# A hybrid encoder layer on one core: the first token tile of the row projection multiplies by the high parts of the weights first and by the low parts behind, with the second tile's first group between

## What is computed

```
h = rms_norm(x, g_pre_mix)
proj = h @ w_in.astype(x.dtype)
qa, ka, va, za, aa, ba, qb, kb, vb = jnp.split(proj, _split_points(IN_SPLITS), axis=-1)
...
mix = jnp.concatenate([o_a, o_b], axis=-1) @ w_out.astype(x.dtype)
x = x + rms_norm(mix, g_post_mix)
h = rms_norm(x, g_pre_ffn)
u = causal_depthwise_conv(h @ w_up.astype(x.dtype), ffn_conv_w) + ffn_conv_b.astype(x.dtype)
gate, val = jnp.split(u, 2, axis=-1)
y = (jax.nn.gelu(gate, approximate=True) * val) @ w_down.astype(x.dtype)
return x + rms_norm(y, g_post_ffn)
```

## Time and profile before

| | us |
|---|---|
| median of 3 runs | 1221.24 |
| lowest and highest | 1220.97, 1221.99 |
| the profiled execution's own time | 1222.27 |
| its span in the trace | 1220.2 |
| PE busy | 1168.4 (96%) |
| DVE busy | 803.5 (66%) |
| ACT busy | 540.3 (44%) |
| POOL busy | 395.1 (32%) |
| mean granted TensorE clock, share of full speed | 0.99 |

### The profile page before, as it was taken

One profiled execution on the slowest core, in us unless ns is written; L12 is line 12 of the kernel. 1 busy time (PEld: TensorE's weight loads), 2 busy tenths in 40 slices (PEclk: granted clock), 3 DMA queues, 4 the chain that ended last, 5 costly groups with the idle time before them and its releaser, 6 DMA issues.

```text
span 1220.2 us, 16966 instructions
## 1 busy us (share of the span) xinstructions
PE 1168.4 (96%) x5964; PEld 987.4 (81%) x5964; DVE 803.5 (66%) x1135; ACT 540.3 (44%) x973; POOL 395.1 (32%) x353
## 2 busy tenths in 40 slices
PE   6999999998899999988699999999999999999997
PEld 5888888887888888876488888888888878888886
DVE  6333345467866677758678787787877867664457
ACT  5221143556355444435455444444444434653451
POOL 1222000211133332223346765557655561000001
PEclk9999999999999999999799999999999999999999
DMA  7322224446232223231144535445355557997613
GB/s 267 127 78 86 68 86 121 143 140 227 82 115 88 92 71 116 64 104 55 69 138 138 188 131 199 168 143 191 130 196 172 173 179 254 363 374 235 191 60 138
DMA packets 118292, 181.85 MB, mean 149 GB/s; under 512 B 20527, under 2 KB 78671, under 8 KB 113999
## 3 DMA queue, kind: packets, MB, share of 16 engines
q1 hardware_dynamic: 118223, 180.94, 44.1%
HBM read 123.21 MB, written 57.70 MB: 148 GB/s over the span
## 4 chain that ended last, share of the span: by engine, by line
PE 48%; DVE 3%; issue 1%; ACT 1%; POOL 0%; DVEq 0%; POOLq 0%; ACTq 0%
PE sums L2912 6%; PE sums L2913 6%; PE sums L2914 6%; PE f_ps_up L2912 6%; PE f_ps_up L2913 5%; PE f_ps_up L2914 5%; PE f_ps_up L2985 3%; PE f_ps_up L2986 3%; PE f_ps_up L2984 3%; PE sums L2986 2%; PE sums L2985 2%; PE sums L2984 2%; DVE h_t L2798 0%; ACT stage L2606 0%; DVE f_rest_raw L2695 0%
## 5 line engine op out<-in xcount | busy, mean ns | idle before, releaser
L2866 POOL TENSOR_TENSOR f_w_raw<-stage 128x512 f32<-128x512 f32 x44 | 69.4, 1578 | 136.5 <-PE f_ps_up L2914 132.8
L2620 DVE TENSOR_TENSOR f_w<-f_w_raw,f_w 128x512 fp32r<-128x512 f32 (+1 forms) x55 | 71.0, 1310 | 23.6 <-POOL f_w_raw L2866 23.5
L2870 POOL TENSOR_TENSOR conv<-conv 128x512 f32<-128x512 f32 x44 | 73.0, 1658 | 16.9 <-DMA conv<-in_w_down 14.3
L222 PE MATMUL sums<-split,slab_w 128*128 128x512 f32 x192 | 75.9, 395 | 0.5 <-PEq L273 0.5
L2870 POOL TENSOR_TENSOR f_conv<-f_conv 128x512 f32<-128x512 f32 x44 | 65.4, 1486 | 32.0 <-DMA y_blocks<-f_conv 28.6
L224 PE MATMUL sums<-split,slab_w 128*128 128x512 f32 x192 | 74.9, 390 | 0.0
L223 PE MATMUL sums<-split,slab_w 128*128 128x512 f32 x192 | 74.7, 389 | 0.0
L2912 PE MATMUL f_ps_up<-split,f_w 128*128 128x512 f32 x176 | 69.5, 395 | 4.4 <-DVEq L2616 3.7
L243 DVE SCALAR_TENSOR_TENSOR conv<-sums,conv_taps,conv 128x1023 f32<-128x1023 f32 (+6 forms) x39 | 46.8, 1199 | 37.3 <-ACT conv L234 36.4
L2913 PE MATMUL f_ps_up<-split,f_w 128*128 128x512 f32 x176 | 69.2, 393 | 0.0
L2914 PE MATMUL f_ps_up<-split,f_w 128*128 128x512 f32 x176 | 69.1, 393 | 0.0
(11 more groups left out here) (410 smaller groups left out, 3462.9 us busy)
## 6 DMA issues: line engine op xcount, KB each, us to landing
stage<-in_w_up SPq DMA_DIRECT2D x22, 1024.0 KB, 6.0
y_blocks<-f_conv SPq DMA_DIRECT2D x22, 1024.0 KB, 4.9
conv<-in_w_down SPq DMA_DIRECT2D x11, 1024.0 KB, 7.3
w_down_sums<-conv SPq DMA_DIRECT2D x11, 1024.0 KB, 10.5
stage<-y_blocks SPq DMA_DIRECT2D x40, 256.0 KB, 5.8
f_rest_raw<-y_blocks SPq DMA_DIRECT2D x37, 256.0 KB, 5.9
x_tile<-in_x SPq DMA_DIRECT2D x12, 512.0 KB, 4.3
stage<-in_w_in SPq DMA_DIRECT2D x6, 1024.0 KB, 6.7
```

Of the source, the lines that this page charges most:

```text
L222: pe.matmul(bank, w_hi, h_hi[:, k, cols], start=(k == 0), stop=False)
L2620: dve.tensor_tensor(out, src, hi.bitcast(F32), ALU.subtract).then_inc(s_lo[name], 1)
L2866: pool.tensor_tensor(raw_sum(m), a, b, op).then_inc(s_add[m], 1)
L2870: pool.tensor_tensor(view(out), view(a), view(b), op).then_inc(signal, 1)
```

## The change

On PE, tile 0 and the whole of tile 1 are taken out of the common loop and written by hand in `first_tiles`. `rows_high` issues, per slice, high by high and low by high (both with the weights' high part); `rows_low` issues high by low for slices whose other two products are done. Group 0 of tile 0: the high products of the four chunks, then the low ones. Group 1: the same, with the transposes of tile 1 moved from ahead of the group into its middle. Then the high products of tile 0's group 2, the high products of tile 1's group 0, the low products of tile 0's group 2, the low products of tile 1's group 0, the transposes of tile 2, and groups 1 and 2 of tile 1, each high first. Tiles 2 to 7 are as before. The number of matmuls and transposes is the same. On POOL, tile 0's two copies also wait for all 11 low parts of the weights.

```
--- before.py
+++ after.py
@@ pool: def tile(t, par, i)
                 if not (isinstance(t, int) and t == T - 1):
                     rstd(t + 1, 1 - par)
+                if isinstance(t, int) and t == 0:
+                    pool.wait_ge(s_wlo, NCH)
                 pool.wait_ge(s_hi, 2 * (t + 1))
                 pool.wait_ge(s_lo, 2 * (t + 1))
@@ pe
-            def tile(t, par, i):
-                pe.wait_ge(s_lo, 1 if isinstance(t, int) and t == 0 else 2 * (t + 1))
+            def rows_high(par, g, ks):
+                bank = row_sums(3 * par + g)[:, 0:GROUPS[g][1]]
+                for k in ks:
+                    pe.matmul(bank, tile_hi[:, par, k], group_w(g, 0)[:, k], start=(k == 0), stop=False)
+                    pe.matmul(bank, tile_lo[:, par, k], group_w(g, 0)[:, k], start=False, stop=False)
+
+            def rows_low(par, g, ks):
+                bank = row_sums(3 * par + g)[:, 0:GROUPS[g][1]]
+                for k in ks:
+                    op = pe.matmul(bank, tile_hi[:, par, k], group_w(g, 1)[:, k], start=False, stop=(k == KD - 1))
+                return op
+
+            def first_tiles():
+                pe.wait_ge(s_lo, 1)
+                for c in range(4):
+                    pe.wait_ge(s_whi, c + 1)
+                    if c == 2:
+                        pe.wait_ge(s_lo, 2)
+                    rows_high(0, 0, range(2 * c, 2 * c + 2))
+                for c in range(4):
+                    pe.wait_ge(s_wlo, c + 1)
+                    op = rows_low(0, 0, range(2 * c, 2 * c + 2))
+                op.then_inc(s_mm, 1)
+                for c in range(4):
+                    if c == 2:
+                        front(1, 1)
+                    pe.wait_ge(s_whi, 5 + c)
+                    rows_high(0, 1, range(2 * c, 2 * c + 2))
+                for c in range(4):
+                    pe.wait_ge(s_wlo, 5 + c)
+                    op = rows_low(0, 1, range(2 * c, 2 * c + 2))
+                op.then_inc(s_mm, 1)
+                for c in range(8, NCH):
+                    pe.wait_ge(s_whi, c + 1)
+                    rows_high(0, 2, range(CHUNKS[c][1], CHUNKS[c][1] + CHUNKS[c][2]))
+                pe.wait_ge(s_lo, 4)
+                pe.wait_ge(s_z, 1)
+                rows_high(1, 0, range(KD))
+                for c in range(8, NCH):
+                    pe.wait_ge(s_wlo, c + 1)
+                    op = rows_low(0, 2, range(CHUNKS[c][1], CHUNKS[c][1] + CHUNKS[c][2]))
+                op.then_inc(s_mm, 1)
+                rows_low(1, 0, range(KD)).then_inc(s_mm, 1)
+                front(2, 0)
+                for g, evicted in ((1, s_mid), (2, s_last)):
+                    pe.wait_ge(evicted, 1)
+                    rows_high(1, g, range(KD))
+                    rows_low(1, g, range(KD)).then_inc(s_mm, 1)
...
             front(0, 0)
-            tiles(pe, tile)
+            first_tiles()
+            with pe.Fori(1, T // 2 - 1) as i:
+                tile(i * 2, 0)
+                tile(i * 2 + 1, 1)
+            tile(T - 2, 0)
+            tile(T - 1, 1)
```

More of the change, by code:

```diff
@@ L657, in front @@
                     last.then_inc(s_tr, 1)
-            def tile(t, par, i):
-                pe.wait_ge(s_lo, 1 if isinstance(t, int) and t == 0 else 2 * (t + 1))
-                for g, (c0, n) in enumerate(GROUPS):
-                    by_chunk = isinstance(t, int) and t == 0 and g < 2
-                    if not by_chunk:
-                        pe.wait_ge(s_wlo, READY[g])
-                    if not (isinstance(t, int) and t == 0):
-                        pe.wait_ge((s_z, s_mid, s_last)[g], t)
+            def rows_high(par, g, ks):
[3 more added lines that the diff above has]
+                    pe.matmul(bank, tile_lo[:, par, k], group_w(g, 0)[:, k], start=False, stop=False)
@@ L667, in tile @@
+            def tile(t, par):
+                pe.wait_ge(s_lo, 2 * (t + 1))
+                for g, (c0, n) in enumerate(GROUPS):
+                    pe.wait_ge((s_z, s_mid, s_last)[g], t)
                     bank = row_sums(3 * par + g)[:, 0:n]
                     for k in range(KD):
-                        if by_chunk and k % 2 == 0:
-                            pe.wait_ge(s_wlo, 4 * g + k // 2 + 1)
-                        if by_chunk and g == 0 and k == KD // 2:
-                            pe.wait_ge(s_lo, 2)
```

## The result

| | before | changed |
|---|---|---|
| median, us | 1221.1 (6 runs) | 1227.66 (6 runs, 1226.09 to 1230.99) |
| ratio, 95% interval | | 1.005 [1.0036, 1.0064] |
| profiled execution, own time and span | 1222.27, 1220.2 | 1230.99, 1229.0 |

The kernel became slower by 6.6 us, against +2.4 forecast; the range ended at 1224.9. Over all 30 runs its median is 1226.1 and its mean 1226.06, from 1222.13 to 1231.39, while the 99 runs of the kernel before that stand beside the first six and beside the experiments e1 to e12 have a mean of 1222.25. So the change costs 3.8 us on average, and the first six runs were slower than most. That it is slower by more than 0.2% holds either way.

A forecast was written before the change was run, and what follows sets the result against it. PE, busy 96% of the span, was taken as the bound, so its waits count. -0.37 - 1.43 - 0.11 + 2.9 + 1.4 = +2.4 us gave a median of 1223.6, range 1221.9 to 1224.9.

The forecast's parts named there:

- Group 0: Tile 0's first group in the row projection: no gain, its 24 matmuls had no wait, ending at 19.01 either way.
- The two waits: PE's waits for low weight parts at tile 0's groups 1 and 2 go: -0.37 and -1.43, with 0.11 of slots -1.91 us.
- POOL's wait: Tile 0's copies wait for the last low part: nothing on the path, DVE up to 1.6 us earlier.
- Tile 2's norm late: Tile 2's transposes wait for `p_h`, held by tile 0's later group end: PE stands 2.9 us, net +1.0.
- The clock: Behind the 2.9 us wait PE's clock falls to 0.50: +1.4 us, between 0 and 1.7.
- The Trainium skill's rule: Gaps under a bound keep the clock; 2.9 us lies just under it: rival B, +1.0, 1222.2, chance 0.14.
- The row of 1.65 us in the earlier trace: Evidence for the clock's fall: behind that wait, at 322.52, the granted clock is 0.50 from 323 on.
- Loop. Nothing: Tiles 2 to 7 keep their code; the step into PE's loop cost no slot before, so no cost.
- goes through to the end: A shift of PE in the row projection reaches the kernel's end, since PE releases the other engines' work behind it.
- A: Rival: clock falls only after PE resumes, low for a whole stretch with matmuls, 1.72: +2.7, 1223.9, chance 0.33.
- D: Rival: two low clock stretches, in the wait and once more after it: +4.2, 1225.4, chance 0.08.
- C: Rival: tile 2's `p_h` is there in time, so the change gives what it removes: -1.9, 1219.3, chance 0.05.

The follow-up runs named there:

- e1: Changed kernel with the low products of tile 0's group 2 again ahead of tile 1's group 0: 1222.63 us against 1222.12, ratio 1.0007.
- e12: Repeat of e5, POOL's new wait alone in the kernel before: 1220.27 us (11 runs), ratio 0.9987.
- e7: The changed kernel run again, nothing altered: 1224.10 us (12 runs), ratio 1.0021.
- e5: Kernel before with only POOL's new wait added, PE's order and loop as before: 1220.90 us (12 runs), ratio 0.9989.
- e8: Changed kernel without POOL's new wait: 1226.52 us (12 runs), ratio 1.0030.
- e9: The kernel before, unchanged, run in the place of a changed one: 1221.86 us (11 runs), ratio 0.9995.
- e10: The changed kernel run a third time, nothing altered: 1226.60 us (12 runs), ratio 1.0036.
- e17: Kernel before with 40 unused semaphore increments at the start of PE's list, no delay: 1221.96 us (11 runs), ratio 1.0000.
- e13: Kernel before with 61 unused semaphore increments at the start of PE's list, which also start PE late: 1228.96 us (6 runs), ratio 1.0046.
- e16: Kernel before with one more wait at PE's start, a delay without added instructions: 1224.45 us (11 runs), ratio 1.0017.
- e14: Changed kernel with 195 unused increments at PE's start, later instructions 512 behind the kernel before; first matmul 21.77 us later: 1245.88 us (5 runs).
- e2: Changed kernel with 13 matmuls nobody reads filling PE's wait before tile 2's transposes: 1226.74 us (6 runs), ratio 1.0036.
- e18: Changed kernel with 40 unused semaphore increments at PE's start, no delay: 1228.05 us (8 runs), ratio 1.0041.

## Why the prediction was wrong

**Group 0: nothing.** Its 24 matmuls again have no wait. It ended at 19.63 instead of 19.01 in this trace and at 18.23 in e7, since the clock's first rise came at another time (first fast matmul at 17.1, 15.8 and 14.3). The kernel before has that scatter too (15.8 and 17.4), so it is not the change's.

**The two waits, -1.91 with the slots: right.** They are gone; e1 shows the gain by itself, 1.57 us at tile 2's first matmul.

**POOL's wait: right in its steps, undervalued.** DVE came 1.6 us earlier, as worked out from 0.76 + 0.85. That this alone gives 1.5 us in the order of before (e5, e12) the prediction never asked, since it weighed the edit only inside of the change. Inside it is worth nothing that can be measured (e8).

**Tile 2's norm late: right, 2.62 us instead of 2.9.** The transposes came 17.55 us behind group 1 instead of 16.60: +0.95, where +1.0 was forecast. The chain of the earlier trace rows repeated itself step by step.

**The clock: +1.4 between 0 and 1.7: both ends occurred.** 1.61 where it fell, 0 where it held (e7, e8), behind waits of equal length. The Trainium skill's rule (TensorE: Matmul & The Clock Gate, section "Why this matters for your kernels"), by which this gap is short enough, is met by two of six traces and broken by four. The row of 1.65 us in the earlier trace rows was the better guide, but as a chance, not as a certainty: at the same place e9, the kernel before again, has the same wait (1.64 us at 322.63) with no fall behind it. With 4 of 6, the projection costs 1.0 us and about 1.1 for the clock, 2.1 together. Four traces of the changed order (changed, e7, e8, e10) have their projection end 1.65 later on average than three of the kernel before (before, e9, e17).

**"Loop. Nothing", and that a shift of PE "goes through to the end": this step failed.** The prediction looked only at whether the branch cost a slot between two matmuls. What leaving the loop did was to make PE's program 317 instructions longer, and so to move all later ones. With that, a fetch of instructions fell into the small round trip of the first delta-rule tile (4.68 us instead of 3.27). In the same four traces the rest of the kernel takes 3.7 us more than before's (1091.1 and 1087.4). Over all 30 runs the whole loss is 3.8, so the profiled executions were among the slower; of it some 2 us are the row projection's, by its mechanism, and some 2 us this; this split is an estimate from the traces, no run has the two apart. None of the rivals had it: A to D were cases of the clock and of the chain in the projection. The range failed by the same step. It gave the runs' own scatter half a us to one, from three runs of the kernel before, and took for granted that the changed program would scatter as little; it scatters over 9 us.

**Rivals.** C (-1.9) is what e1 shows in the projection, where the between order is left out. A, the whole of a low stretch with matmuls under it, is the nearest to the first trace. D, two low stretches in a row, was not seen in the projection.

**What stays open.** Shown is that the offset of PE's instructions decides (e13 against e16 with the loop kept, e14 with the tiles written out), and that by it an instruction packet falls among the packets of the small store or not; that is also why 40 is harmless there and 61 is not. A long trip is 1.2 to 1.8 us of a loss that in five traces (changed, e2, e8, e13, e18) is 5.3 us or more; e1 has the long trip and lost only 2.2 against the 1087.4. Whether the rest of the loss comes from the lower clock behind the longer waits (in four of the six traces with a long first trip it fell near 251) or from elsewhere is not shown. That the 41 to 43 packets are PE's is inferred from their number: 10684 and 11001 instructions are 41.7 and 43.0 blocks of 256. Only one kernel, e13, has the loss without the hand-written tiles.

## What to carry to other kernels

Moving work of tile 1 ahead of the last part of tile 0 moves the end of tile 0, and with it everything that the other engines make only after it: follow that chain before counting the waits that go. Take apart an edit that does several things: here one line of it, a wait on POOL that keeps its copies from running beside DVE, was worth 1.5 us by itself, and the whole edit cost 3.8. And when code is unrolled or instructions are added, look at the scatter of the runs and at where the instruction packets fall against short transfers that an engine waits for, not only at the stage that was edited; their number alone says little (43 packets in e14, and no loss). Shifting the later code by empty instructions in an idle stretch tells whether its position matters.

## What the runs showed that was not expected

- 61 empty instructions at the head of PE's list cost 3.5 to 4.5 us more than a delay of the same length (e13, e16), while 40 cost nothing (e17, ratio 1.0000).
- One instruction packet of 16384 bytes among the 512 packets of a small store made the store and load round trip 4.5 to 5.1 us instead of 3.2 to 3.4 (first tile, 6 and 9 traces).
- An increment of a semaphore took PE 0.16 to 0.17 us (behind 61 of them the first transposes started at 10.27 us, behind 195 at 30.71).
- Behind a wait of 2.62 us the clock fell in four traces and held in two, of nearly the same program.
- One program's executions can differ by 9 us (30 runs, 1222.13 to 1231.39) while those of a near twin differ by 5 (99 runs of the kernel before, 1220.57 to 1225.71).
